# 64 of 256 tokens leave the dense expert layers; their experts' rows are gathered by indirect DMAs

## The reference

```python
expert = (e1 * N_KEYS + e2).reshape(T, PEER_HEADS * PEER_TOPK)      # 256 x 128
gate = jax.nn.softmax(best, axis=-1).reshape(T, PEER_HEADS * PEER_TOPK)
u = jnp.take(u_tab, ec, axis=0)                                     # per token 128 rows of 2048
act = jax.nn.gelu(jnp.einsum('cd,ckd->ck', hc, u), approximate=False) * gc
vv = jnp.take(v_tab, ec, axis=0)
out = jnp.einsum('ck,ckd->cd', act, vv)
# then x = x + out, and a last rmsnorm
```

## Time and profile before

| | us |
|---|---|
| median of 3 runs | 3631.59 |
| lowest and highest | 3631.08 to 3645.18 |
| profiled execution, first to last instruction (the only time given for it) | 3639.5 |

### The profile page before, as it was taken

One profiled execution on the slowest core, in us unless ns is written; L12 is line 12 of the kernel. 1 busy time (PEld: TensorE's weight loads), 2 busy tenths in 40 slices (PEclk: granted clock), 3 DMA queues, 4 the chain that ended last, 5 costly groups with the idle time before them and its releaser, 6 DMA issues.

```text
span 3639.5 us, 70287 instructions
## 1 busy us (share of the span) xinstructions
PE 3480.2 (96%) x24838; PEld 2995.8 (82%) x24838; DVE 2464.0 (68%) x4354; ACT 1600.8 (44%) x2512; POOL 36.4 (1%) x49
## 2 busy tenths in 40 slices
PE   8999899999999899988888998999999999999998
PEld 6888788888888777777777886888888888888887
DVE  6767686767777786766656589656565656565666
ACT  5445444444444455433334214445454535353543
POOL 0000000000000000000000001000000000000000
PEclk9999999999999999999999999999999999999999
DMA  5544455555555444400025444565656565565554
GB/s 195 169 144 162 150 182 177 187 167 195 172 191 173 154 145 145 136 12 9 9 80 170 155 143 172 185 212 182 213 183 217 187 214 195 199 206 194 203 192 150
DMA packets 165850, 593.84 MB, mean 163 GB/s; under 512 B 18448, under 2 KB 26768, under 8 KB 164432
## 3 DMA queue, kind: packets, MB, share of 16 engines
q1 hardware_dynamic: 159744, 559.14, 46.4%
q0 software_dynamic: 5968, 32.77, 2.5%
HBM read 572.70 MB, written 18.87 MB: 163 GB/s over the span
## 4 chain that ended last, share of the span: by engine, by line
PE 88%; DVE 8%; ACT 2%; issue 1%; DMA 1%; DVEq 0%; SPq 0%; ACTq 0%; POOLq 0%
PE bank L584 50%; PE bank L585 25%; PE bank L920 5%; PE bank L1204 2%; DVE hot_row L2766 1%; PE bank L1241 1%; DVE w_lo L1878 1%; DVE hot_col L2761 1%; PE bank L605 1%; DVE proj L2436 1%; PE bank L891 0%; ACT w_hi L1278 0%; PE bank L865 0%; DMA gates<-g_stage 0%; DVE acc L1944 0%
## 5 line engine op out<-in xcount | busy, mean ns | idle before, releaser
L584 PE MATMUL bank<-h_two,w_hi 128*128 128x512 f32 x5360 | 1894.6, 398 | 49.5 <-DVE h_two L1936 20.4
L585 PE MATMUL bank<-h_two,w_lo 128*128 128x256 f32 x5360 | 1501.1, 280 | 0.0
L1878 DVE TENSOR_TENSOR w_lo<-raw,w_hi 128x1024 fp32r<-128x1024 f32 (+1 forms) x1054 | 1228.6, 1185 | 231.9 <-ACT w_hi L1278 230.1
L1278 ACT ACTIVATE w_hi<-raw 128x1024 fp32r<-128x1024 f32 (+1 forms) x1054 | 1045.9, 1024 | 533.8 <-PE bank L585 494.2
L584 PEld LDWEIGHTS bank<-h_two,w_hi 128*128 128x128 f32 x5360 | 1008.5, 188 | 296.5 <-issue 38.8
L585 PEld LDWEIGHTS bank<-h_two,w_lo 128*128 128x128 f32 x5360 | 1014.8, 189 | 1.1 <-issue 0.7
L584 PE MATMUL bank<-p_two,w_hi 128*128 128x512 f32 x1792 | 627.2, 395 | 2.8 <-DVE acc L1903 1.8
L585 PE MATMUL bank<-p_two,w_lo 128*128 128x256 f32 x1792 | 500.7, 279 | 0.0
L584 PEld LDWEIGHTS bank<-p_two,w_hi 128*128 128x128 f32 x1792 | 335.9, 187 | 84.9 <-DVE p_two L2780 5.5
L585 PEld LDWEIGHTS bank<-p_two,w_lo 128*128 128x128 f32 x1792 | 338.0, 189 | 0.0
L1899 DVE TENSOR_TENSOR acc<-acc,bank 128x256 f32 x192 | 80.9, 421 | 369.4 <-PE bank L585 369.4
(11 more groups left out here) (382 smaller groups left out, 3031.6 us busy)
## 6 DMA issues: line engine op xcount, KB each, us to landing
raw<-in_u_tab SPq DMA_DIRECT2D x256, 512.0 KB, 4.1
raw<-in_v_tab SPq DMA_DIRECT2D x256, 512.0 KB, 4.3
raw<-in_w_up SPq DMA_DIRECT2D x176, 512.0 KB, 4.4
raw<-in_w_in SPq DMA_DIRECT2D x174, 512.0 KB, 3.8
raw<-in_w_out SPq DMA_DIRECT2D x64, 512.0 KB, 4.2
raw<-in_w_down SPq DMA_DIRECT2D x64, 512.0 KB, 3.5
raw<-in_w_pq SPq DMA_DIRECT2D x32, 512.0 KB, 4.5
gates<-g_stage POOLq DMA_DIRECT2D x16, 896.0 KB, 5.7
```

The lines of the kernel that those rows point to most:

```text
L584: nc.tensor.matmul(o[:], wh, pair.rearrange("p a t -> p (a t)"), start=(k == 0), stop=False)
L585: last = nc.tensor.matmul(o[:, T:2 * T], wl, pair[:, 0, :], start=False, stop=(k == nk - 1))
L1278: nc.scalar.activation(w_hi[c % 2][:, at:end], raw[c % 2][:, at:end], ACT.Copy).then_inc(hi_done, 1)
L1878: nc.vector.tensor_tensor(w_lo[c % 2][:, at:end], raw[c % 2][:, at:end], w_hi[c % 2][:, at:end].bitcast(F32), ALU.subtract).then_inc(lo_do ...
```

## The change

`TD` = 192 tokens stay in the dense layers; the last `TG` = 64 take another way. Every chunk of the dense expert stages is called with `width=TD`: matmuls of 384 and 192 columns, and 192-element elementwise operations. Rounds of gate products: 48. `g_stage` no longer holds group 0.

For the 64 tokens, two partitions each (`KQ` = 2) take 64 of the token's 128 experts. Their activations are turned (`by_token`, 16 small f32 matmuls on TensorE, copied by ScalarE to `h_tok`), expert numbers and gates are put beside them by POOL's DMAs. Then 64 indirect DMAs gather one row of `u_rows` for each of 128 partitions (2048 floats, 1.05 MB each), VectorE multiplies each by `h_tok` and sums to a dot product; Gelu and gates follow; then 64 gathers of `v_rows`, each scaled and added to `y_tok`. Two buffers `rows`. The 128 VectorE operations are put into the 14 stages from first layer 1 to second layer 6, by `OPS_IN`, each behind a pair of chunks. At the end 16 small matmuls sum the two partitions of each token and turn the sum, and it is added to x. The loops of VectorE and POOL in the dense stages are written out. `cst2_loaded` is merged with `s_cst`.

```diff
+TD = 192
+TG = T - TD
+KQ = P // TG
+GATHERS = SLOTS // KQ
+OPS_IN = (8, 8, 8, 8, 8, 8, 8, 8, 8, 13, 8, 13, 8, 14)
+ROWS_USED = [sum(OPS_IN[:i]) for i in range(len(OPS_IN) + 1)]
...
-                    nc.tensor.matmul(o[:], wh, pair.rearrange("p a t -> p (a t)"), start=(k == 0), stop=False)
-                    last = nc.tensor.matmul(o[:, T:2 * T], wl, pair[:, 0, :], start=False, stop=(k == nk - 1))
+                    nc.tensor.matmul(o[:, 0:2 * width].rearrange("p (a t) -> p a t", a=2), wh, pair[:, :, 0:width],
+                                     start=(k == 0), stop=False)
+                    last = nc.tensor.matmul(o[:, width:2 * width], wl, pair[:, 0, 0:width], start=False,
+                                            stop=(k == nk - 1))
...
             for x in range(3, EARLY):
                 whole_tiles(x, 0, DT)
+                if x in (3, 5):
+                    by_token(x - 3)
+                    by_token(x - 2)
...
+            def sums_turned():
+
+                pe.wait_ge(rows_used, 2 * GATHERS)
+                for t in range(DT):
+                    last = nc.tensor.matmul(bank[7 - t // 8][:, t % 8 * TG:(t % 8 + 1) * TG], y_tok[:, t * P:(t + 1) * P],
+                                            count[:, P + 3 * K_TOP:P + 3 * K_TOP + TG], start=True, stop=True)
+                last.then_inc(peer_turned, 1)
...
                 expert_values(N_PEER + 2 * DT, g, p_two)
+            sums_turned()
             expert_values(N_PEER + DT, PEER_G - 1, h_two)
...
+            act.wait_ge(rows_used, GATHERS)
+            nc.scalar.activation(act_of[:], dots[:], ACT.Gelu).then_inc(gate_exp, 1)
+            with act.Fori(4, PEER_G - 2) as g:
...
+            pool.wait_ge(turned_copied, 4)
+            for q in range(1, KQ):
+                pool.dma_start(h_tok[TG * q:TG * (q + 1), :], h_tok[0:TG, :]).then_inc(k_swapped, 16)
+            pool.wait_ge(slots_done, 3)
+            for q in range(KQ):
+                to, of = slice(TG * q, TG * (q + 1)), slice(GATHERS * q, GATHERS * (q + 1))
+                pool.dma_start(expert_of[to, :], tok_expert[P - TG:P, of]).then_inc(k_swapped, 16)
+                pool.dma_start(gate_of[to, :], tok_gate[P - TG:P, of]).then_inc(k_swapped, 16)
...
+            def gather(n):
+
+                if n == 0:
+                    pool.wait_ge(k_swapped, 32 + (3 * KQ - 1) * 16)
+                    pool.wait_ge(half_done, 2 * (N_PEER + DT))
+                if n >= 2:
+                    pool.wait_ge(rows_used, n - 1)
+                of = n % GATHERS
+                nc.gpsimd.indirect_dma_start(
+                    out=rows[n % 2][:], out_offset=None, in_=a["u_rows" if n < GATHERS else "v_rows"],
+                    in_offset=bass.IndirectOffsetOnAxis(ap=expert_of[:, of:of + 1], axis=0)
+                ).then_inc(rows_loaded[n % 2], 16)
...
-            with pool.Fori(1, PEER_G) as g:
+            begun = 2
+            for g in range(1, PEER_G):
+                while begun < 2 * GATHERS and begun < ROWS_USED[2 * g - 1] + 2:
+                    gather(begun)
+                    begun += 1
 
                 pool.wait_ge(stage_used, g * DT + S_PEER)
-                pool.dma_start(g_now[:], gates_d[bass.ds(g, 1)].rearrange("a p t e -> (a p) t e")
-                               ).then_inc(g_loaded, 16)
+                pool.dma_start(g_now[:], gates_d[g]).then_inc(g_loaded, 16)
...
+            def gathered_rows(n):
+
+                dve.wait_ge(rows_loaded[n % 2], 16 * (n // 2 + 1))
+                got, of = rows[n % 2][:], n % GATHERS
+                if n < GATHERS:
+                    last = nc.vector.tensor_tensor_reduce(got, got, h_tok[:], 1.0, 0.0, ALU.mult, ALU.add,
+                                                          dots[:, of:of + 1])
+                else:
+                    dve.wait_ge(rows_used, n)
+                    if of == 0:
+                        dve.wait_ge(best_ready, 2)
+                        last = nc.vector.tensor_scalar(y_tok[:], got, act_of[:, 0:1], None, ALU.mult)
+                    else:
+                        last = nc.vector.scalar_tensor_tensor(y_tok[:], got, act_of[:, of:of + 1], y_tok[:],
+                                                              ALU.mult, ALU.add)
+                last.then_inc(rows_used, 1)
+
+            def rows_behind(x, i):
+
+                at = ROWS_USED[x]
+                for n in range(at, ROWS_USED[x + 1]):
+                    if (n - at) * 8 // OPS_IN[x] == i:
+                        gathered_rows(n)
...
                     for j in range(2):
-                        add_lower(N_PEER + DT + j, g * DT + i * 2 + (C_PEER + j + 1), stage[j][:])
+                        add_lower(N_PEER + DT + j, g * DT + i * 2 + (C_PEER + j + 1), stage[j][:, 0:TD], TD)
                         gated(i, j, g)
                         lower(N_PEER + DT + j + 2, g * DT + i, whole=WHOLE)
-                        gated_lower(i, j, g, tile_of(p_hi, i * 2 + j), tile_of(p_lo, i * 2 + j))
+                        gated_lower(i, j, g, p_hi[:, i * 2 + j, :], p_lo[:, i * 2 + j, :])
+                    rows_behind(2 * g, i)
...
+            for g in range(PEER_G - 2):
+                first_layer(g)
+                for i in range(DT // 2):
                     for j in range(2):
                         second_layer(N_PEER + 2 * DT, g, i, j)
+                    rows_behind(2 * g + 1, i)
```

More of the change, by code:

```diff
@@ L570, in _, with chunk @@
         def _(pe):
-            def chunk(c, it, two, nk=DT, per_tile=None, whole=0):
+            def chunk(c, it, two, nk=DT, per_tile=None, whole=0, width=T):
                 n = it * 2 + (c - whole)
@@ L1223, in _, with by_token @@
                 scores3(u)
+            def by_token(part):
+                if part >= 2:
+                    pe.wait_ge(turned_copied, part - 1)
+                for k in range(4):
+                    last = nc.tensor.matmul(bank[(2, 7)[part % 2]][0:TG, k * P:(k + 1) * P],
+                                            h_f32[:, 4 * part + k, TD:T], ident, start=True, stop=True)
+                last.then_inc(peer_turned, 1)
             for x in range(3, EARLY):
                 whole_tiles(x, 0, DT)
+                if x in (3, 5):
+                    by_token(x - 3)
+                    by_token(x - 2)
             pe.wait_ge(slots_done, 1)
@@ L1232, in _ @@
                     if u % 4 == 3 or u == 5:
-                        last.then_inc(slots_turned, 1)
-            pe.wait_ge(turned_copied, 2)
-            for n in range(T // 4):
+                        last.then_inc(peer_turned, 1)
+            pe.wait_ge(turned_copied, 6)
+            for n in range(TD // 4):
                 pe.wait_ge(hot_ready, n + 1)
@@ L1858, in _ @@
             nc.gpsimd.memset(acc[:], 0.0).then_inc(acc_zero, 1)
-            for b in range(T // 16):
+            pool.wait_ge(turned_copied, 4)
[6 more added lines that the diff above has]
+                pool.dma_start(gate_of[to, :], tok_gate[P - TG:P, of]).then_inc(k_swapped, 16)
@@ L1868, in _ @@
+            for n in range(2):
+                gather(n)
+            for j in range(2):
+                pool.wait_ge(gates_stored[j], 16 * (TD // 32))
+            begun = 2
[3 more added lines that the diff above has]
+                    begun += 1
                 pool.wait_ge(stage_used, g * DT + S_PEER)
-                pool.dma_start(g_now[:], gates_d[bass.ds(g, 1)].rearrange("a p t e -> (a p) t e")
-                               ).then_inc(g_loaded, 16)
+                pool.dma_start(g_now[:], gates_d[g]).then_inc(g_loaded, 16)
@@ L1872, in _ @@
+            while begun < 2 * GATHERS:
+                gather(begun)
+                begun += 1
         @block.vector
@@ L2754, in _ @@
                                     ).then_inc(slots_done, 1)
-            dve.wait_ge(turned_copied, 2)
+            own = slice(P - TG, P)
+            nc.vector.scalar_tensor_tensor(tok_expert[own, :], slot[own, 0, TT - 1, :], float(P), slot[own, 1, TT - 1, :],
+                                           ALU.mult, ALU.add).then_inc(slots_done, 1)
+            dve.wait_ge(slots_done, 1)
+            nc.vector.tensor_copy(tok_gate[own, :], slot[own, 2, TT - 1, :]).then_inc(slots_done, 1)
+            dve.wait_ge(turned_copied, 6)
             dve.wait_ge(sub_loaded, 32)
-            for n in range(T // 4):
+            for n in range(TD // 4):
                 if n >= 2:
@@ L2821, in _ @@
                     second_layer(N_PEER + 2 * DT, g, i, j)
-                    gated_lower(i, j, g + 1, tile_of(h_hi, i * 2 + j), tile_of(h_lo, i * 2 + j))
+                    gated_lower(i, j, g + 1, h_hi[:, i * 2 + j, 0:TD], h_lo[:, i * 2 + j, 0:TD])
+                rows_behind(2 * g + 1, i)
             g = PEER_G - 1
+            dve.wait_ge(peer_turned, 7)
+            for k in range(2):
+                own = xT[:, 8 * k:8 * k + 8, TD:T]
```

(5 more changed lines are left out.)

170 lines of the change are left out of this document (97 added, 73 removed).

## The result

The changed kernel takes 3608.9 us (median of 5 runs, 3605.5 to 3622.8). The kernel before, run beside it on the same chip, takes 3641.4 us: ratio 0.9928, 95% interval 0.9901 to 0.9956. Faster, as forecast, but by 0.7% where 2.5% was forecast: 3609 lies outside the forecast's own range of 3525 to 3580 and far from 3541; it is inside the wider one, 3500 to 3620, whose upper end rival B had set. The profiled execution has a span of 3606.8 us, where the sum gave 3549 (3639.5 less 91). So 58 us are to be found.

The account below looks back on a forecast made before the run. TensorE was taken to bound the kernel, 88% of the chain of waits. Terms summed to -90.9 us on a 3639.5 us span; 91 off the median 3631.6 gave 3541 us, own range 3525 to 3580, 8 in 10 from 3500 to 3620.

Parts of the forecast that it names:

- rival B: Groups 4 to 6: gathers land late, 14 us after issue, adding 75 us, for 3616 us; chance 0.20.
- An ordinary second layer: Expert second layers with 8 gathers: 26.8 MB at 394 GB/s take 68 us, hidden under TensorE.
- The two signs that I had named for being wrong: Expert stages: first layers getting shorter, or the narrow matmul not at its floor, would show the forecast wrong.
- TensorE at 192 columns: Dense expert matmuls: weight floor of 0.112 us, 0.2845 us a pair, 4.55 a chunk, 72.8 a stage.
- Rival A: Narrow matmul falls back to plain f32 pace: 0.497 us a pair, 4163 us in all; chance 0.12.
- rival C: Narrow matmul has no weight floor: 0.2595 us a pair, 3509 us in all; chance 0.20.
- My sign for it: TensorE's timeline: each narrow matmul starts 0.112 us before the next matmul.
- VectorE's ring in first layers: First layers: closed VectorE loop of 4.77 us a chunk; two chunks with a row operation 11.8 us; +35 us.
- Groups 0 to 3: Second layers: TensorE binds, 73.5 us each with 0.7 for the seam, VectorE idle; -64.5 us.
- Groups 4 and 5: Second layers with 13 gathers: DMA last, 32.0 MB in 81 us, 2 x 82 against 178.4; -14.4 us.
- Group 6: Second layer: 95 us against 92.8, +2; then waits and 16 f32 products before group 7's second layer, +8.
- Gate products and seam: Gate-product stage: 86 us instead of 119.5, -33.5; ahead of it -6; first expert matmul near 2240.

Follow-up runs that it names:

- few_bytes: The changed kernel with gathers from the third on replaced by plain 32 KB loads from a fixed place, all row operations kept: ratio 0.9742, span 3552.2 us.
- both_out: The changed kernel with 32 KB plain loads for gathers from the third on and row operations on 64 of 2048 columns: ratio 0.9373, span 3416.0 us.
- ops_second_only: The changed kernel with no row operations in first layers, 16 to 22 in each second layer instead: ratio 1.0174, span 3709.5 us.
- The pieces test: The changed kernel with gathers split in two (ratio 0.9974), the gates load split in three (0.9892), or both (0.9945).

## Why the prediction was wrong

The step that failed is "An ordinary second layer moves 16.8 + 8.4 + 1.6 = 26.8 MB, 68 us: hidden", and with it "so DMA is last there: 2 x 82". I divided a stage's bytes by the rate of full engines, and took what came out under TensorE's time as hidden. But loads are due chunk by chunk, 1.05 MB every 4.55 us, and POOL's bytes come in bursts: where a gather and the gates load meet, the weights get 0.54 MB in 6 us, and one load is 5.69 us late for ScalarE. The engines were 88 and 91% busy over the stages of groups 0 and 2 at 332 and 331 GB/s. few_bytes prices the gathered bytes at 54.8 us; the forecast had given them some 5 (164 us for groups 4 and 5, which take 159 without them). So they make up some 50 of the 58 us. Without them the kernel takes 3552.2 where the forecast less 5 is 3544: the other 8 us are the points below, with both signs.

The rate was wrong for a whole stage as well. 430 GB/s were reached, but for 6 us; over the second layers of groups 0, 2, 4 and 5 it was 329 to 333 GB/s at a share of 0.87 to 0.91, 364 to 378 if full, and not 394. By group 4's 366 the forecast's 32.0 MB are 87 us, an estimate; 90.6 were measured. The two signs that I had named for being wrong didn't come: the first layers got longer, and the narrow matmul is at its floor. What missed was the sign for groups 0 to 3, 73 to 74 us.

Point by point:

- *TensorE at 192 columns: right.* The weight loads of the changed kernel at 2700, then its matmuls (start, duration, instruction):

```profile
2700.06 0.19 PEld L608 LDWEIGHTS bank<-p_two,w_hi 128*128 128x128 f32 x1
2700.17 0.19 PEld L610 LDWEIGHTS bank<-p_two,w_lo 128*128 128x128 f32 x1
2700.34 0.19 PEld L608 LDWEIGHTS bank<-p_two,w_hi 128*128 128x128 f32 x1
```

```profile
2700.14 0.36 PE L608 MATMUL bank<-p_two,w_hi 128*128 128x384 f32 x1
2700.34 0.25 PE L610 MATMUL bank<-p_two,w_lo 128*128 128x192 f32 x1
2700.43 0.36 PE L608 MATMUL bank<-p_two,w_hi 128*128 128x384 f32 x1
```

The pair takes 0.284 us and a chunk 4.55 us. Rival A (0.497) and rival C (0.2595) fall. My sign for it was wrong: the narrow matmul starts 0.09 us before the next, and the floor of 0.11 us stands between the weight loads, at 2700.06 and 2700.17. Loads run ahead, so the wide matmul's start is what moves.
- *VectorE's ring in first layers: right.* From the add at 3398.76 to the row operation at 3403.54 it takes 4.78 us (4.77 was forecast), on VectorE's timeline of the changed kernel, here with the row operation behind it:

```profile
3398.76 0.35 DVE L1980 TENSOR_TENSOR stage<-stage,bank 128x192 f32<-128x192 f32 x1
...
3400.99 2.36 DVE L1970 TENSOR_TENSOR w_lo<-raw,w_hi 128x1024 fp32r<-128x1024 f32 x2 [1.48 <-ACT w_hi L1325]
3403.27 0.35 DVE L2905 TENSOR_TENSOR p_two<-p_raw,p_two 128x192 fp32r<-128x192 f32 x1
3403.54 2.35 DVE L2886 SCALAR_TENSOR_TENSOR h_tok<-rows,act_of,h_tok 128x2048 f32<-128x2048 f32 x1
```

  Two chunks take 11.76 us against 11.8, seven stages 662.1 against 660. That the sum fits so well is in part luck: the bytes are 7.6 us of it, and without them the seven stages take 654.4, since the first chunks of a stage aren't held by the ring.
- *Groups 0 to 3: the failed step,* +19.5 us; few_bytes takes back 15.3, both_out the rest. The floor and the seam were right: 73.4 a stage in both_out against 73.5.
- *Groups 4 and 5: rightly put on DMA, wrongly sized.* 91 us a stage, not 82. Without the bytes they would take 79 and 80 instead of the 74 of VectorE's sum, which I put down to operations that come in pairs. The 358 GB/s a core of the Trainium skill ("DMA: Bandwidth & Descriptors", section "Specifications") gave 89 us and comes closer; but it isn't a ceiling for this core: 430 GB/s over 6 us. Whether the 333 and 329 GB/s of these stages come from loads that wait for each other or from slower transfers isn't shown.
- *Group 6: 103 was forecast, 118.7 came.* 8.6 us are the bytes, 5.4 the sums, which were mis-sized as well; 1.7 aren't assigned. The changed kernel's TensorE timeline, and its windows of TensorE's idle stretch, of the sums, and of the matmuls after them:

```profile
3510.76 7.09 PE L1304 MATMUL bank<-count,h_tok 128*128 128x64 f32 x32 [6.60 <-DVE h_tok L2886]
```

```profile
3504.10:3510.60 6.50, 0.06 (x1) 0.00 (x0) 6.50 (x9) 1.42 (x2) 0.00 (x0) 0.83 0.81 236
3510.80:3517.50 6.70, 6.70 (x32) 6.70 (x32) 0.00 (x0) 0.00 (x0) 0.00 (x0) 0.50 0.30 115
3517.60:3522.00 4.40, 4.40 (x19) 4.40 (x18) 1.77 (x3) 0.00 (x0) 0.00 (x0) 0.50 0.00 0
```

  TensorE idles 6.60 us for the last row operation (5.75 less 1.4 hidden was forecast), and the granted clock falls to half, 1.2 GHz, so the 32 records run at 0.215 us each instead of 0.112: 6.9 us, not 3.6. Together 13.4 us where I had 8, and the last stage starts at half the clock, which is its 75.0 for 73. I had the clock in the working only for first layers' gaps.
- *Rival B: fell as the cause, but it is real.* 16.0 us of waits for rows in the whole kernel; in ops_second_only 162 us, 65.1 of them between 2990 and 3445, in the stages of groups 4 and 5. Its 3616 lies near the measured time by luck: the time was lost on weight loads.
- *Gate products and seam: right,* first expert matmul 2241.1 against 2240.

Open: what share of few_bytes' gain comes from the packet split and what from plain volume. The pieces test moved the delay from one queue to the other instead of taking it away. Weights in larger packets were not tried. Nor was a kernel with the full bytes in plain loads: few_bytes took the indirection away with the bytes. For the bytes speak the DMA rows, in which POOL's queue fills the engines; that the rest costs nothing is argued, not shown.

## What to carry to other kernels

Bytes hidden on a stage's average are not hidden when they come in bursts on a second queue, least of all where two of its transfers meet: work out what each buffer's load gets in the few us before it is due, with the other queue's packets at their size. Before work is moved off TensorE, measure the floor of its narrow matmul; with f32 weights nothing is gained below it. And move only as much as fits under the engine that binds, where it fits: 32 tokens, with their operations in the second layers alone, won 107 us where 64 in both layers won 33.
